# Three narrow products in place of a wide and a narrow one, in the first MLP matrix

## The reference, cut to what matters

```
def squared_relu_mlp(h, w_in, w_out):           # h [256, 2048]
    return jnp.square(jax.nn.relu(h @ w_in)) @ w_out   # w_in [2048, 8192], w_out [8192, 2048]
```

## Time and profile before

| | |
|---|---|
| median of three runs | 1896.06 us |
| profiled execution: first to last instruction (its span) | 1893.8 us |
| what lies around the span, against the median | 2.3 us |
| TensorE matmuls busy | 1883.6 us, 99% |
| TensorE weight loads busy | 1589.2 us, 84% |
| VectorE busy | 1581.6 us, 84% |
| ScalarE busy | 999.9 us, 53% |
| m1 steps (L791 and L792) | 400.0 to 1024 us, 1024 each |

### The profile page before, as it was taken

How to read it: one execution, slowest core, us unless ns; L and a number is a source line. 1 busy time by engine, 2 the same in 40 slices (tenths; PEclk the granted TensorE clock), 3 DMA queues, 4 the chain that set the end, 5 groups by cost and what they waited for, 6 DMA issues and landing times.

```text
span 1893.8 us, 24873 instructions
## 1 busy us (share of the span) xinstructions
PE 1883.6 (99%) x9230; PEld 1589.2 (84%) x9230; DVE 1581.6 (84%) x2169; ACT 999.9 (53%) x1455; POOL 136.2 (7%) x88
## 2 busy tenths in 40 slices
PE   9999999999999999999999999999999999999999
PEld 7888888888888888888888878888888788888887
DVE  6898888888888888888887568898898688888986
ACT  6646555454444444443444454667655555667562
POOL 1241233000000000000000000001100000010000
PEclk9999999999999999999999999999999999999999
DMA  7787877888888898989897556655556466555554
GB/s 262 261 282 247 289 261 250 279 289 300 294 298 299 298 301 291 309 289 303 283 320 245 189 157 177 196 170 159 154 201 200 144 192 180 166 169 162 199 191 144
DMA packets 259195, 445.04 MB, mean 235 GB/s; under 512 B 16051, under 2 KB 123461, under 8 KB 258819
## 3 DMA queue, kind: packets, MB, share of 16 engines
q1 hardware_dynamic: 258643, 443.36, 72.1%
q10 hardware_dynamic: 432, 0.09, 0.0%
HBM read 441.27 MB, written 2.11 MB: 234 GB/s over the span
## 4 chain that ended last, share of the span: by engine, by line
PE 99%; DVE 1%; issue 0%; ACT 0%; POOL 0%; DVEq 0%; ACTq 0%
PE P L733 73%; PE P L791 13%; PE P L792 6%; PE P L505 2%; PE P L636 1%; PE P L635 1%; PE P L621 0%; PE P L572 0%; PE P L547 0%; PE P L643 0%; PE P L718 0%; PE P L653 0%; PE P L654 0%; PE P L652 0%; PE P L573 0%
## 5 line engine op out<-in xcount | busy, mean ns | idle before, releaser
L1148 ACT ACTIVATE WH<-RAW 128x1024 fp32r<-128x1024 f32 (+1 forms) x647 | 669.4, 1046 | 565.5 <-PE P L733 225.8
L1179 DVE TENSOR_TENSOR WL<-RAW,WH 128x1024 fp32r<-128x1024 f32 (+1 forms) x649 | 791.5, 1226 | 201.5 <-ACT WH L1148 199.4
L733 PE MATMUL P<-WH,AHL 128*128 128x512 f32 (+1 forms) x2048 | 643.1, 390 | 3.4 <-DVE AHL L1179 3.2
L733 PEld LDWEIGHTS P<-WH,AHL 128*128 128x128 f32 x2048 | 382.4, 188 | 79.8 <-issue 4.7
L733 PE MATMUL P<-WL,AHL 128*128 128x512 f32 (+1 forms) x1024 | 392.6, 385 | 0.0
L791 PE MATMUL P<-AHL,WH 128*128 128x512 f32 x1024 | 360.5, 398 | 0.0
L733 PE MATMUL P<-WH,BH 128*128 128x512 f32 x896 | 351.1, 392 | 0.0
L733 PE MATMUL P<-WH,BL 128*128 128x512 f32 x896 | 348.9, 389 | 0.0
L733 PE MATMUL P<-WL,BH 128*128 128x512 f32 x896 | 348.8, 389 | 0.0
L792 PE MATMUL P<-AHL,WL 128*128 128x256 f32 x1024 | 282.5, 281 | 0.0
L1176 DVE SCALAR_TENSOR_TENSOR ADA<-RAW,CC,ADA 128x1024 f32<-128x1024 f32 x180 | 236.7, 1315 | 0.1
(11 more groups left out here) (270 smaller groups left out, 1391.8 us busy)
## 6 DMA issues: line engine op xcount, KB each, us to landing
RAW<-in_ada_w_dram SPq DMA_DIRECT2D x192, 512.0 KB, 5.2
RAW<-in_mlp_w_in_dram SPq DMA_DIRECT2D x128, 512.0 KB, 4.7
RAW<-in_mlp_w_out_dram SPq DMA_DIRECT2D x128, 512.0 KB, 5.3
RAW<-in_sb_w_qkv_dram SPq DMA_DIRECT2D x95, 512.0 KB, 5.2
RAW<-in_w_in_dram SPq DMA_DIRECT2D x80, 512.0 KB, 3.9
RAW<-in_w_in_dram SPq DMA_DIRECT2D x128, 256.0 KB, 3.1
RAW<-in_w_out_dram SPq DMA_DIRECT2D x64, 512.0 KB, 4.2
RAW<-in_sb_w_o_dram SPq DMA_DIRECT2D x32, 512.0 KB, 5.6
```

What stands on the lines that cost most here:

```text
L733: return e.matmul(P[:, 2 * u.pair + t, 0:u.w], x, w, start=u.first and k == 0 and part == 0, stop=u.last and k == u.nk - 1 and part == 2)
L1148: e.activation(WH[:, n % NH, 0:size], RAW[:, i % NR, 0:size], ACT.Copy).then_inc(w_high, 1)
L1179: return e.tensor_tensor(o, x, h.bitcast(F32), ALU.subtract)
```

## The change

`turned_unit` makes three matmuls of 256 columns a step (WH with AH, WL with AH, WH with AL), all added up in the left half of the bank. ScalarE's eviction applies Relu to that half and releases the banks; VectorE's part is one product of HID with itself. HID shrinks to two buffers and the tally `hid_part` goes. In `h_pair` the same data are addressed in two dimensions instead of one.

```
 turned_unit
-  w, o, kt = slice(...), P[:, 2 * u.pair + i, :], u.k0 + k
+  w, o, kt = slice(...), P[:, 2 * u.pair + i, 0:256], u.k0 + k
   last = u.last and k == u.nk - 1
-  both = lambda: e.matmul(o.rearrange("p (x n) -> p x n", x=2), WH[:, s, w], AHL[:, :, kt, :], start=u.first and k == 0, stop=last, skip_group_check=True)
-  lower = lambda: e.matmul(o[:, 0:256], WL[:, s, w], AH[:, kt, :], start=False, stop=False, skip_group_check=True)
-  for f in (lower, both) if last else (both, lower):
-      m = f()
+  e.matmul(o, WH[:, s, w], AH[:, kt, :], start=u.first and k == 0, stop=False)
+  e.matmul(o, WL[:, s, w], AH[:, kt, :], start=False, stop=False)
+  m = e.matmul(o, WH[:, s, w], AL[:, kt, :], start=False, stop=last)

 hid_evict, ScalarE
   wait_chunk("m1", c)
   if c > 1:
-      e.wait_ge(*emptied("m1", c - 2))
+      e.wait_ge(*hid_sq.at(c - 2))
   p = 2 * opened["m1", c][0]
-  e.activation(HID[:, c % 2, :, :], P[:, p:p + 2, 256:512], ACT.Copy).then_inc(*hid_part.up(c))
+  e.activation(HID[:, c % 2, :, :], P[:, p:p + 2, 0:256], ACT.Relu).then_inc(pair_emptied[opened["m1", c][0]], 1)

 hid_evict, VectorE
-  p = 2 * opened["m1", c][0]
-  v = HID[:, 2 + c % 2, :, :]
-  e.wait_ge(*hid_part.at(c))
-  e.tensor_tensor(v, P[:, p:p + 2, 0:256], HID[:, c % 2, :, :], ALU.add).then_inc(pair_emptied[opened["m1", c][0]], 1)
+  v = HID[:, c % 2, :, :]
   e.wait_ge(*emptied("m1", c))
-  fma(FB[:, c % 2, :], flat(v), 0.0, flat(v), ALU.max, ALU.mult).then_inc(*hid_sq.up(c))
+  e.tensor_tensor(FB[:, c % 2, :], flat(v), flat(v), ALU.mult).then_inc(*hid_sq.up(c))

 h_pair, ScalarE and VectorE
-  e.activation(flat(AH[:, 2 * i:2 * i + 2, :]), f, ACT.Copy)...
+  e.activation(AH[:, 2 * i:2 * i + 2, :], pair(f), ACT.Copy)...
-  low(flat(AL[:, 2 * i:2 * i + 2, :]), f, flat(AH[:, 2 * i:2 * i + 2, :]))...
+  low(AL[:, 2 * i:2 * i + 2, :], pair(f), AH[:, 2 * i:2 * i + 2, :])...
```

More of the change, by code:

```diff
@@ L151, in build @@
         ACC2 = put("ADA", [128, 2, 1024], off=oS + 44 * K)
-        HID = put("HID", [128, 4, 2, 256], off=oS + 16 * K)
+        HID = put("HID", [128, 2, 2, 256], off=oS + 16 * K)
         VR = put("VR", [128, 3, 128], off=oS + 24 * K)
@@ L457, in build @@
         lnexp, tn_mask, a_exp, a_mask, bh_high = tally("sb_log"), tally("sb_neg"), tally("sb_exp"), tally("sb_att"), tally("att_high")
-        rstd_sq, hid_part, hid_sq, hid_high, hid_low = tally("rstd_squared"), tally("hid_low_part"), tally("hid_square"), tally("hid_high"), tally("hid_low")
+        rstd_sq, hid_sq, hid_high, hid_low = tally("rstd_squared"), tally("hid_square"), tally("hid_high"), tally("hid_low")
         pads, tabs, sig = tally("pads"), tally("tables"), tally("sigmoid")
@@ L469, in build @@
         tallies = [un_r, tn_high, tn_low, first_h, first_l, x_begun, sel, ada_t, ada_r, gate_t, taps_t, cols, c_act, angle_d, angle_a, sq_sum, ms, rstd, x_high, x_end, x_gated, h_high, h_low, scl, qk_sq, qk_ms, qk_done, qk_red,
-                   lnexp, tn_mask, a_exp, a_mask, bh_high, rstd_sq, hid_part, hid_sq, hid_high, hid_low, pads, tabs, sig, lat_sq, lat_ms, lat_r, lat_high,
+                   lnexp, tn_mask, a_exp, a_mask, bh_high, rstd_sq, hid_sq, hid_high, hid_low, pads, tabs, sig, lat_sq, lat_ms, lat_r, lat_high,
                    kr_sq, kr_ms, kr_rot, q_sq, q_ms, q_rstd, q_rot, rot, k_sq, k_ms, k_rs, k_nrm, k_rope, rope_zero, x_scaled, x_scaled_a, mx, ex, rcp, o_high, conv_d, x_mid, p_bias, p_gated,
@@ L481, in build @@
         flat = lambda ap: ap.rearrange("p a b -> p (a b)")
+        pair = lambda ap: ap.rearrange("p (k n) -> p k n", k=2)
         tiles = lambda ap: ap.rearrange("p (a b) -> p a b", b=128)
@@ L788, in turned_unit @@
                     for i in range(2):
-                        w, o, kt = slice(k * 256 + i * 128, k * 256 + (i + 1) * 128), P[:, 2 * u.pair + i, :], u.k0 + k
+                        w, o, kt = slice(k * 256 + i * 128, k * 256 + (i + 1) * 128), P[:, 2 * u.pair + i, 0:256], u.k0 + k
                         last = u.last and k == u.nk - 1
-                        both = lambda: e.matmul(o.rearrange("p (x n) -> p x n", x=2), WH[:, s, w], AHL[:, :, kt, :], start=u.first and k == 0, stop=last, skip_group_check=True)
-                        lower = lambda: e.matmul(o[:, 0:256], WL[:, s, w], AH[:, kt, :], start=False, stop=False, skip_group_check=True)
-                        for f in (lower, both) if last else (both, lower):
-                            m = f()
+                        e.matmul(o, WH[:, s, w], AH[:, kt, :], start=u.first and k == 0, stop=False)
+                        e.matmul(o, WL[:, s, w], AH[:, kt, :], start=False, stop=False)
+                        m = e.matmul(o, WH[:, s, w], AL[:, kt, :], start=False, stop=last)
                 return m
@@ L994, in h_pair @@
                 e.wait_ge(*T.emptied(name))
-                e.activation(flat(AH[:, 2 * i:2 * i + 2, :]), f, ACT.Copy).then_inc(*h_high.up(l, "pair", i))
+                e.activation(AH[:, 2 * i:2 * i + 2, :], pair(f), ACT.Copy).then_inc(*h_high.up(l, "pair", i))
             def z_evict(l, c):
@@ L1395, in h_pair @@
                 e.wait_ge(*h_high.at(l, "pair", i))
-                low(flat(AL[:, 2 * i:2 * i + 2, :]), f, flat(AH[:, 2 * i:2 * i + 2, :])).then_inc(*h_low.up(l, "pair", i))
+                low(AL[:, 2 * i:2 * i + 2, :], pair(f), AH[:, 2 * i:2 * i + 2, :]).then_inc(*h_low.up(l, "pair", i))
             def pads_(l):
```

## The result

The changed kernel takes 1903.86 us (median of four runs, 1903.82 to 1904.12); the kernel before 1895.89 (median of four, 1895.21 to 1897.71). The ratio is 1.0040, with a 95% interval of 1.0028 to 1.0052: slower by 8.0 us, and clear of no change.

What follows compares the result with a forecast made beforehand. TensorE's instruction count times pace was taken to bound m1. Three products at 120.0 ns against 353.2 ns a step, x 1024, gave +7.0 us, all other terms 0: 1896.06 + 7.0 = 1903.1 us, range 1894.4 to 1909.

Steps and rivals of the forecast that it cites:

- What bounds: In m1, time is TensorE's instruction count times their pace; no waits at its products, so faster engines beside it give nothing.
- 120.0 ns for a 256-column product: In m1: 106.7 ns for columns plus 13.4 fixed; three make 360.0 ns a step against 353.2, +7.0 us in all.
- The old step gives 6.6 ns back: Old m1 step costs 353.2 ns, not 346.7, because the wide product reads AH and AL in two places; that cost goes.
- Loads fit below 120 ns: 1024 more weight loads, each holding its port at most 112 ns by a burst of twelve 128-column matmuls: cost 0.
- VectorE's relief is worth 0: VectorE loses m1's addition, 22.1 us, and its fused product becomes plain; nothing of TensorE in m1 waits for it: 0.
- ScalarE, table, release, new wait, h_pair, transfers: Relu for Copy, possible function-table loads, bank release, ScalarE's wait for hid_sq, h_pair's addressing and DMA: each taken as 0.
- Sum: Whole kernel: profiled span 1893.8 + 7.0 = 1900.8 us; median 1896.06 + 7.0 = 1903.1 us.
- Rival 1: In m1, no cost: narrow product runs at 117 to 118 ns, -2.3 to +0.8 us, about 1895.3; 14%.
- Rival 2: In m1, instruction or weight supply becomes the bound: +48 us (1944) at 133.4 ns a product, +89 at 146.7; 7%.
- Rivals 3 and 4: Faster, by m1 products at the loads' pace or by VectorE's relief (5.8 us at most, outside m1); 6% together.
- Rival 3: In m1, products fall to the loads' 112 ns: 336 ns a step, -17.6 us, 1878.5; 6% with rival 4.

Runs made afterwards that it cites:

- split, in m2: Kernel before with every 512-column product of the second MLP matrix (m2) split into two of 256, m1 as before: 1914.53 us against 1896.03 (1.0098).
- the halved kernel: Changed kernel with its third product (WH with AL) in two of 128 columns, four products and loads a step: 2009.62 us against 1896.20 for the kernel before.
- grouped: Kernel before with each m1 unit's eight wide products first, then its eight narrow ones (reversed in a chunk's last unit): 1891.33 us against 1896.03 (0.9976).
- the run with the products alone: Kernel before with three 256-column products, high x low in the bank's right half, both evictions as before: 1903.46 us against 1896.20 (1.0038).
- in pairs: Kernel before with m1's products ordered wide, wide, narrow, narrow in every row block: 1892.01 us against 1896.03 (0.9979).

## Why the prediction was right, and where its working was not

- *What bounds*: right. m1 lengthened by 7.3 us and its products waited for nobody, before and after. A group of four chunks took 45.19 us before and 46.07 after, which over eight groups is the 7.0 forecast; the 0.3 more lie in the first eight chunks, which have no m2 between them and where the old step took 352.4 ns (81.77 us for 232 steps up to 491.5 us).
- *120.0 ns for a 256-column product*, extrapolated from 320, 384 and 512 columns: right, 0.120 in the changed kernel and, split, in m2. The fixed part of 13.4 ns a product is what the change pays. Whether it belongs to the product, to its load or to the change from one to the next stays open, as each product has its load; that it isn't there in every surrounding is shown by the 0.06 us of a 128-column product in the halved kernel, where columns and fixed part would make 66.7 ns.
- *The old step gives 6.6 ns back*: the size was right (360.0 - 353.2 is what the sum needed), the reason was wrong. I put it down to the wide product's two places; one place changed nothing. It is the price of mixing widths: in rows of one width products keep 120 and 227 ns. In the kernel before, by the trace's own nanoseconds (its views round to 10), the distances behind the wide products are 233, 241 and 236 in turn and those behind the narrow ones 117, 120 and 113, so 10 more on average for the wide and only 3.3 less for the narrow. The error did no harm to the sum only because the new step has no mixed widths either, and it hid that the old step could be had cheaper: with the same two products, grouped, it is 4.7 us faster than before and some 12.5 faster than the changed kernel.
- *Loads fit below 120 ns*: right in the outcome, but the row behind it could not show it, and the 4 ns of room that there were are luck. In the halved kernel loads stood 115 to 116 ns apart, more than the "at most 112". The burst of the earlier trace rows is of another kind: KV and PTB are plain float32 (both are allocated without the type fp32r), and products of plain float32 cost about twice as much a column (0.84 ns against 0.42). In the kernel before, four of 256 columns (from TTr, plain too) start 0.215 us apart:

```profile
1248.52 0.60 PE L635 MATMUL P<-TTr 128*128 128x256 f32 x2
1248.95 0.59 PE L636 MATMUL P<-TTr 128*128 128x256 f32 x2
1249.38 0.27 PE L635 MATMUL P<-TTr 128*128 128x128 f32 x1
```

By that pace a 128-column one takes about 108 by itself, so the burst's 112 was mostly the products' own time and said little on the loads of fp32r weights.
- *VectorE's relief is worth 0*: right, by the run with the products alone: the same time with the old eviction. Its busy time fell by 18.0 us, not 22: the 22.1 of the addition went, but the 180 instructions of L1176 on ADA rose from a mean of 1315 to 1326 ns and the 480 on CA from 476 to 479, 3.4 us together; why isn't known. A plain product of 0.684 was expected and 0.692 came.
- *ScalarE, table, release, new wait, h_pair, transfers*: no sign of any of them in the rows. They were not tried one by one; together with the eviction they are within the 0.4 us between the changed kernel and the one with the products alone (which has the old `h_pair` too).
- *Sum*: 7.0 forecast, 8.0 measured; of the profiled span's 8.2, 7.3 lie in m1 and the other 0.9 outside it (0.8 ahead of m1). The spans of the kernel before differ by more than that among themselves: 1893.1 to 1895.4 us in the 15 runs measured beside the last experiments.
- *Rival 1* (117 to 118 ns): such values exist, but only for a narrow product among wide ones. *Rival 2*: 60 ns an instruction was sustained throughout m1, so neither the supply nor the loads are the limit there; one of the two is, 4 to 5 ns a product further down. By the formula of the Trainium skill ("TensorE: Matmul & The Clock Gate", section "Back-to-back issue gap"), which the page gives for isolated matmuls, one more product would have cost 2.5 ns; the rows say 13.3 for these products with a load each, so the measurement decides against the figure here. *Rivals 3 and 4*: not seen. Rival 3 took its 112 ns from the same burst of plain float32.

## What to carry to other kernels

Where TensorE is never idle, count products as well as columns: each one costs its columns and a fixed part, and adding up all three products in one place saves only another engine's time, which was worth nothing here. Read the pace from the starts of equal neighbours in long rows, and extrapolate; a product too short for its weight load pays the pair's time (here about 115 ns). Take such a bound only from rows of the same type of operands. If widths must differ, put equal widths together, and before you name a cause for a leftover of a few nanoseconds, try it: the edit that it suggests may do nothing while its neighbour gains.

## What the runs showed that I had not expected

- A change of width leaves a trace in the pace of the products behind it. Eight wide ones behind eight narrow ones take 1.84 us and not 1.81; alternating one by one costs 6.5 ns a step (353.2 against 346.7); in pairs the step costs 4.2 ns less than that, in whole units 4.5 less (0.54 and 0.57 us over a group's 128 steps). What in the chip does this, and why pairs are almost as good as eights, stays open: no run here looks inside it.
- The pattern of a mixed row is not only its own: the same m1 code ran at 45.02 us a group behind rows of 256 columns, and 45.2 behind rows of 512.
- With less than about 115 ns of columns between loads on average, the loads go on evenly and the products bunch: 0.06 and 0.17 us apart in the same step.
